# Third mixer's first stage: four chunks' block-diagonal products in one block behind every fourth projection

## The reference, cut to what matters

```python
x_in, z = jnp.split(h @ w_in, 2, axis=-1)                 # 2 x 2048 columns
x_pad = jnp.pad(x_in, ((0, 0), (ML_CONV - 1, 0), (0, 0)))
conv = sum(x_pad[:, tap:tap + S] * conv_w[tap] for tap in range(ML_CONV))
x_conv = jax.nn.silu(conv + conv_b)
q = headwise(x_conv, w_q)      # block-diagonal, blocks of 4 x 4
k = headwise(x_conv, w_k)
v = headwise(x_in, w_v)
gates = (jnp.concatenate([q, k, v], axis=-1) @ w_if + b_if)
```

## Time and profile before

| | before |
|---|---|
| median of 3 runs | 932.74 us |
| profiled execution, span from first to last instruction | 930.8 us |
| TensorE busy | 920.5 us (99%) |
| VectorE busy | 696.6 us (75%) |
| ScalarE busy | 549.3 us (59%) |
| mean granted clock of TensorE | 0.999 |

### The profile page before, as it was taken

The page is one execution under the profiler, slowest core; times in us unless marked ns, Lnnn a source line. Parts: engine busy times, 40 slices in busy tenths (PEclk is TensorE's granted clock), DMA queues, the critical chain, the costliest instruction groups (busy, mean ns, idle before and its releaser), DMA issues.

```text
span 930.8 us, 16812 instructions
## 1 busy us (share of the span) xinstructions
PE 920.5 (99%) x6163; PEld 814.0 (87%) x6163; DVE 696.6 (75%) x1250; ACT 549.3 (59%) x965; POOL 84.6 (9%) x105
## 2 busy tenths in 40 slices
PE   9999999999999999999999999999999999999997
PEld 8999888888888987888888888999889789999985
DVE  4978777767666777677766777998687987678875
ACT  5654465545455677656545546765554745477783
POOL 0000011111110000100000000000011005622300
PEclk9999999999999999999999999999999999999999
DMA  8665557766665332767666653543231676423312
GB/s 317 215 204 175 192 173 235 229 214 200 203 201 196 107 119 89 231 225 231 205 195 182 185 192 119 168 152 129 82 107 49 205 280 195 142 84 107 121 42 91
DMA packets 43726, 157.94 MB, mean 170 GB/s; under 512 B 5464, under 2 KB 6248, under 8 KB 42896
## 3 DMA queue, kind: packets, MB, share of 16 engines
q1 hardware_dynamic: 41520, 147.79, 49.2%
q0 software_dynamic: 1856, 8.58, 2.5%
q10 hardware_dynamic: 288, 0.72, 0.2%
HBM read 155.63 MB, written 1.05 MB: 168 GB/s over the span
## 4 chain that ended last, share of the span: by engine, by line
PE 90%; DVE 4%; ACT 3%; DMA 2%; issue 1%; SPq 0%; DVEq 0%; ACTq 0%
PE ps L760 15%; PE ps L545 9%; PE ps L546 8%; PE ps L547 8%; PE ps L758 8%; PE ps L600 7%; PE ps L602 7%; PE ps L604 7%; PE ps L755 2%; PE ps L1154 2%; DMA raw<-stream_dram 2%; PE ps L1103 1%; PE ps L1129 1%; PE ps L756 1%; ACT wh L1240 1%; PE ps L583 1%
## 5 line engine op out<-in xcount | busy, mean ns | idle before, releaser
L1784 DVE TENSOR_TENSOR wl<-raw,wh 128x1024 fp32r<-128x1024 f32 x270 | 331.0, 1232 | 98.1 <-ACT wh L1408 48.9
L1240 ACT ACTIVATE wh<-raw 128x1024 fp32r<-128x1024 f32 x174 | 182.3, 1058 | 93.6 <-DMA raw<-stream_dram 77.9
L760 PE MATMUL ps<-hxa,wh 128*128 128x512 f32 x616 | 219.5, 396 | 0.0
L545 PE MATMUL ps<-hxa,wh 128*128 128x256 f32 x672 | 196.6, 293 | 0.9 <-DVE wl L1784 0.4
L546 PE MATMUL ps<-hxa,wh 128*128 128x256 f32 x672 | 189.9, 283 | 0.0
L547 PE MATMUL ps<-hxa,wl 128*128 128x256 f32 x672 | 189.8, 282 | 0.0
L758 PE MATMUL ps<-hxa,wl 128*128 128x256 f32 x616 | 171.9, 279 | 0.0
L545 PEld LDWEIGHTS ps<-hxa,wh 128*128 128x128 f32 x672 | 128.3, 191 | 10.0 <-issue 7.0
L760 PEld LDWEIGHTS ps<-hxa,wh 128*128 128x128 f32 x616 | 115.6, 188 | 23.9
L1408 ACT ACTIVATE wh<-raw 128x1024 fp32r<-128x1024 f32 x96 | 101.6, 1058 | 59.1 <-PE ps L760 21.9
L546 PEld LDWEIGHTS ps<-hxa,wh 128*128 128x128 f32 x672 | 128.6, 191 | 0.1
(11 more groups left out here) (370 smaller groups left out, 1347.9 us busy)
## 6 DMA issues: line engine op xcount, KB each, us to landing
raw<-stream_dram SPq DMA_DIRECT2D x271, 512.0 KB, 4.1
biasm<-bias_dram POOLq DMA_DIRECT2D x12, 192.0 KB, 4.2
w<-w_dram POOLq DMA_DIRECT2D x1, 2048.0 KB, 10.8
mlw<-mlw_dram POOLq DMA_DIRECT2D x1, 1056.0 KB, 7.0
x<-x_dram SPq DMA_DIRECT2D x1, 1024.0 KB, 7.4
mem<-memT_dram SPq DMA_DIRECT2D x1, 1024.0 KB, 8.3
memx<-mem_dram SPq DMA_DIRECT2D x1, 1024.0 KB, 5.8
grow<-rows_dram POOLq DMA_DIRECT2D x2, 512.0 KB, 4.2
```

The source lines that it names most:

```text
L545: pe.matmul(o, wh[:, w_s, w_cols], act[hi], start=start, stop=False, skip_group_check=True)
L760: return pe.matmul(o, wh[:, s % RING, wc], hx[:, k, :, :], start=False, stop=(k == KC - 1), skip_group_check=True)
L1240: act.activation(wh[:, v % RING, :], raw[:, v % RAW, :], ACT.Copy).then_inc(wh_ready, 1)
L1784: dve.tensor_tensor(wl[:, s % RING, :], raw[:, s % RAW, :], wh[:, s % RING, :].bitcast(F32), ALU.subtract).then_inc(wl_ready, 1)
```

## The change

The 16 calls of `chunk` between projections become four blocks. TensorE projects inputs up to c = 6 with nothing between them, and then at c = 6, 10, 14 and 18 does four chunks in a row: score product and values for each, and then the gate sums of all four (`gate_sums`, two sets of four matmuls). `xpad` holds eight inputs, so that four can wait for their block while four more are taken; VectorE waits for `v_done` from c = 8 on, by groups. ScalarE copies the four score products in iteration 6, 10, 14 and 18, behind that iteration's high half and xconv, and then the values. `centre` moves from c = 6 (before the convolution), 10, 14, 18 to c = 7, 11, 15, 19. `gsel` moves to another place, and the two z chunks that are projected early are kept in other slots (`z_of`), to make room.

```diff
@@ -260,7 +260,7 @@
         C = region(17792)
         Dr = region(16384)
         E = region(16384)
-        F = region(12 * 384 * 4)
+        F = region(12 * 384 * 4 + 96)
 
         y = place("y", A, [P, 8, 2, T], F32R)
         ajunk = place("ajunk", A, [P, D])
@@ -306,8 +306,8 @@
         g8 = place("g8", C + 8704, [P, 3 * ML_CH, 8])
         mbd = place("mbd", A + 8192, [P, ML_CH, P])
         bdv = place("bdv", F, [P, ML_CH, P])
-        xpad = place("xpad", F + 8192, [P, 4, T + 3])
-        gsel = place("gsel", F + 12352, [P, 36])
+        xpad = place("xpad", F + 8192, [P, 8, T + 3])
+        gsel = place("gsel", C + 17408, [P, 36])
         cacc = place("cacc", C + 16384, [P, T])
         xconv = place("xconv", B, [P, ML_CH, T])
         mq = place("mq", C, [P, ML_CH, T])
@@ -330,7 +330,7 @@
         h_w = place("h_w", F + 4096, [P, 2, 512])
         zlo = place("zlo", xsq_at, [P, 8, T])
         zhi = place("zhi", F + 8192, [P, 8, T])
-        zpre = place("zpre", F + 16384, [P, 2, T])
+        zpre = place("zpre", F + 16480, [P, 2, T])
         gq = place("gq", A, [P, T])
         h_p = place("h_p", std_at, [P, T])
 
@@ -446,7 +446,7 @@
         def z_of(c):
             if c < 2:
                 return zpre[:, c, :]
-            return zlo[:, c, :] if c < 8 else zhi[:, c - 8, :]
+            return zlo[:, c % Z_EARLY[0], :] if c < 8 or c in Z_EARLY else zhi[:, c - 8, :]
 
 
         NEEDS = {}
@@ -858,24 +858,22 @@
                 if c >= 2:
                     pe.wait_ge(qk_copied, c - 1)
                 pe.matmul(ps[:, c % 2, 0:T], mbd[:, c, :], xconv[:, c, :], start=True, stop=True).then_inc(qk_ready, 1)
-                if c % 4 == 0:
-                    return
-                if c % 4 == 1 and c > 1:
+                if c % 4 == 0 and c > 0:
 
                     pe.wait_ge(v_centred, c // 4)
-                for cv in (c - 1, c) if c % 4 == 1 else (c,):
-                    for st in range(2):
-                        pe.matmul(ps[:, (2, 7)[st], cv % 4 * P:cv % 4 * P + P],
-                                  xpad[:, cv % 4, 3 + st * P:3 + st * P + P], bdv[:, cv, :], start=True, stop=True)
-                if c % 2 == 0:
-                    return
-
-                for q in range(4):
-                    j, cq = q % 2, c - 1 + q // 2
-                    mm = pe.matmul(ps[32 * q:32 * q + 32, 3, 0:T], gw8[:, j, cq, :],
-                                   (xconv[:, cq, :], xpad[:, cq % 4, 3:T + 3])[j], start=(c == 1),
-                                   stop=(c == ML_CH - 1))
-                mm.then_inc(v_done, 2)
+                for st in range(2):
+                    pe.matmul(ps[:, (2, 7)[st], c % 4 * P:c % 4 * P + P],
+                              xpad[:, c % 8, 3 + st * P:3 + st * P + P], bdv[:, c, :], start=True, stop=True)
+
+            def gate_sums(h):
+
+                for i in range(2):
+                    for q in range(4):
+                        j, c = q % 2, 4 * h + 2 * i + q // 2
+                        mm = pe.matmul(ps[32 * q:32 * q + 32, 3, 0:T], gw8[:, j, c, :],
+                                       (xconv[:, c, :], xpad[:, c % 8, 3:T + 3])[j], start=(h == 0 and i == 0),
+                                       stop=(h == ML_HEADS - 1 and i == 1))
+                mm.then_inc(v_done, 4)
 
             for c in range(ML_CH + 3):
                 if c < ML_CH:
@@ -892,8 +890,10 @@
                 if c == 3:
 
                     pe.wait_ge(proj_taken, PM["z", Z_EARLY[1]].n + 1)
-                if c >= 3:
-                    chunk(c - 3)
+                if c >= 6 and c % 4 == 2:
+                    for b in range(c - 6, c - 2):
+                        chunk(b)
+                    gate_sums(c // 4 - 1)
 
 
             def ml_scores(h):
@@ -1561,9 +1561,10 @@
                             .then_inc(x1_ready, 1)
                 if c >= 3:
                     b = c - 3
-                    act.wait_ge(qk_ready, b + 1)
-                    act.activation(mq[:, b, :], ps[:, b % 2, 0:T], ACT.Copy).then_inc(qk_copied, 1)
                     if b % 4 == 3:
+                        for q in range(b - 3, b + 1):
+                            act.wait_ge(qk_ready, q + 1)
+                            act.activation(mq[:, q, :], ps[:, q % 2, 0:T], ACT.Copy).then_inc(qk_copied, 1)
                         act.wait_ge(v_done, b + 1)
                         for st in range(2):
                             act.activation(mvt[:, st, 512 * (b // 4):512 * (b // 4) + 512], ps[:, (2, 7)[st], :],
@@ -2178,11 +2179,10 @@
                 e.then_inc(v_centred, 1)
 
 
-            for b in range(4):
-                dve.memset(xpad[:, b, 0:3], 0.0)
+            dve.memset(xpad[:, :, 0:3], 0.0)
             for c in range(ML_CH + 4):
                 if c < ML_CH:
-                    xp = xpad[:, c % 4, :]
+                    xp = xpad[:, c % 8, :]
                     ch = PM["x", c]
                     if c == 0:
                         invert2(Q_FINAL1)
@@ -2201,12 +2201,10 @@
                     elif c >= 3:
                         ahead(ch.u)
 
-                        if c >= 4:
-                            dve.wait_ge(v_done, c - 3)
+                        if c >= 8:
+                            dve.wait_ge(v_done, c // 4 * 4 - 4)
                         take_from(ch.u, ch.bank, xp[:, 3:T + 3], Rm)
                     dve.wait_ge(proj_taken, ch.n + 1)
-                    if c == 6:
-                        centre(0)
                     if c >= 1:
                         dve.wait_ge(xconv_ready, c)
                     link(dve.tensor_scalar(cacc[:], xp[:, 0:T], col("mlconv", c), None, ALU.mult))
@@ -2221,8 +2219,8 @@
                         take(PM["z", Z_EARLY[1]], z_of(Z_EARLY[1]), Rm)
                     if c < 2:
                         ahead(PM["z", Z_EARLY[c]].u)
-                if c >= 7 and (c - 3) % 4 == 3:
-                    centre((c - 3) // 4)
+                if c >= 7 and c % 4 == 3:
+                    centre((c - 7) // 4)
                 if ML_CH <= c < ML_CH + 2:
 
                     ahead(PM["z", c - ML_CH].u)
```

## The result

| | before | after |
|---|---|---|
| median | 932.78 us (4 runs, 932.65 to 932.87) | 947.24 us (4 runs, 945.55 to 948.89) |
| profiled execution, span | 930.8 us | 943.8 us (its run took 945.55) |
| mean granted clock of TensorE | 0.999 | 0.993 (the other runs 0.991, 0.994, 0.991) |
| ratio to before, 95% interval | | 1.0153 (1.0139 to 1.0168) |

The account below looks back on a forecast made before the run. TensorE bounds, VectorE close behind: waits of 5.0 + 1.9 + 1.9 + 0.1 less 1.2 of switches, plus rounding, give 7.9; 930.8 + 7.9 = 938.7 span, plus 1.94 to the median, 940.6 us. Own range 939.6 to 941.8; wide range 938.6 to 944.2.

Parts of the forecast that it names:

- What bounds: 575 to 665 us: TensorE and VectorE run side by side, TensorE a little slower; a group takes 16.54 against 15.0 us.
- The saved switches: TensorE's gate sums: one return and one entry fewer per group, 0.29 us each group, 1.2 us in four.
- the set in the middle: Gate sums: a set that follows another was taken as 0.48 us, against 0.57 for one alone.
- The turned order of three engines: Chunk 2's score product waits for ScalarE's copies, held behind input 5's convolution; the stage ends 7.9 us later.
- Forecast stalls 5.0, 1.9, 1.9: TensorE's waits for ScalarE's score copies in the first three blocks, in us.
- The 0.1 us for the bank of input 6: Before the first block, TensorE waits about 0.1 us for the bank VectorE frees by taking input 3.
- the one on the clock: First block: if TensorE's clock halves in the stall, 0 to 2.8 us more, up to 943.4 us.
- likeliest (0.47): Whole kernel: the forecast's own range of 939.6 to 941.8 us, without the slow-clock cost, chance 0.47.
- the first stall: First block, chunk 2: TensorE waits 5.0 us, from 604.6 to 609.65, for ScalarE's first score copy.
- The row it rested on: Kernel end: the clock fell at about 928.4 us, 3.6 us behind TensorE's last matmul at 924.76.
- The price, 2.8 us: First block: the 2.8 us of work left would run at half rate, costing 2.8 us at most.
- its rivals: Other totals: clock falls 943.4 (0.31), only switches count 931.5 (0.03), first stall only 936.6 (0.09), dearer gate set and hand-overs 942.8 (0.10).

Follow-up runs that it names:

- the clock held up: The changed kernel with idle matmuls ahead of TensorE's waits in the first three blocks (22, 8 and 8): 941.12 us, ratio 1.0095.
- the first stall filled: The changed kernel with 22 idle matmuls ahead of TensorE's wait in the first block only: 944.76 us, ratio 1.0116.
- late copies alone: The kernel before, with only ScalarE's copies of the score products moved to every fourth iteration: 955.64 us, ratio 1.0231.

## Why the prediction was wrong

**What bounds: right.** TensorE and VectorE side by side, and a wait of either is a loss.

**The saved switches: right, a little low.** Forecast 0.29 per group, measured 0.34; the set in the middle costs 0.43, the upper bound of the prediction, not 0.48.

**The turned order of three engines: right in place, mechanism and size.** Forecast stalls 5.0, 1.9, 1.9, measured 4.8, 1.9, 1.9; with the clock held up, the stage is 8.05 us longer in the profile and the median is 8.0 us over before, where 7.9 was forecast. The 0.1 us for the bank of input 6 was too low: it was 0.7 in the changed kernel's profile, and in some others nothing. Four places for the products or earlier copies take it all away.

**The step that failed is the one on the clock**, in two ways. The forecast took as likeliest (0.47) that it stays up in the first stall; it fell in it in both profiled runs that left that stall open. The row it rested on said so: a fall 3.6 us behind the last matmul and a stall of 5.0. The price, 2.8 us, was right (2.8 and 2.7 against the same block with the stalls filled). And the prediction priced one fall and no more: a fall behind the stalls of 1.9 us stands in neither its sum nor its rivals, without a reason given. In the changed kernel's profile the third block lost 1.6 us to a second fall behind just such a stall. A smaller miss came on top: in that execution TensorE began the stage 0.2 us earlier than before (575.55 against 575.75), but VectorE took input 3 0.5 us later (600.04 against 599.56), and TensorE waited 0.7 us for that bank. The stage grew by 8.05 + 2.84 + 1.58 + 0.68 = 13.15 us.

The Trainium skill, "TensorE: Matmul & The Clock Gate", section "HAM oscillation — how this bites in real kernels", was right where the forecast gave it only 0.31: it expects a burst behind a long enough idle gap to start at half clock. Both profiled first stalls agree (clock 0.50 from about 609 us). The waits in that section's example are 3 to 5 us; the fall behind 1.9 us is this case's own row.

**What stays open.** The profile explains 13.0 us, of a run of 945.55; the median is 1.7 us higher, with clocks of 0.991 in two of the other three runs. That may be a third fall in the stage, or a wait for GpSimd with a fall behind it, as the profile with the first stall filled has at 815 us; only the first run has a profile, so it stays open. When a wait of 1.8 to 1.9 us brings the clock down was not settled: of the seven in these profiles, three did and four did not. Nor was it settled what makes TensorE wait for GpSimd in some executions, or the spread of the kernel before on the later chips, of which no profile was taken.

## What to carry to other kernels

When work is batched on one engine, follow each wait inside the batch to the queue of the engine that ends it: here the first copy of a block came to stand behind a convolution that ended about 5 us after TensorE needed the bank, though the matmuls of the batch were the same. A stall of TensorE costs its length and then the restart, so price the clock with it, and more than once if it repeats. Separate the saving from its means: the gate sums could be put together without moving the products, and only that half was faster.

## What the runs showed of the hardware that was not expected

- The granted clock fell to half behind a stall of 1.9 us, in a stretch in which TensorE had worked without a gap before (third block, 0.50 in 650 to 652 us), and came back within about 4 us of work; it also fell behind two of three waits of 1.8 us for GpSimd (at 805 us with four places, at 815 us with the first stall filled), and stayed up in the other four waits of this length. It fell in all five waits of 3.75 to 7.8 us (the first stall twice, late copies alone three times).
- Gate sums on four column groups cost 0.57 us for a set that stands alone and 0.43 for one that follows another, plus 0.20 for the first projection matmul behind a run of them.
- 38 idle matmuls in TensorE's stalls made the changed kernel about 6 us faster by medians and its stage 5.1 us shorter in the profiles, though the score product of chunk 2 still followed ScalarE's first copy (a start at 609.43 us against 608.98).
- Profiles of these kernels differ by up to 5 us behind the stage, where none of the edits touches the program (276.3 to 281.4 us), so a stage is best compared by its own start and end.
